# Loads moved twelve slots ahead, residual sums moved to VectorE, whole columns moved to ScalarE at the seams of a two-block transformer kernel

## The reference

```python
for i in range(DEPTH):                                  # DEPTH = 2
    need_ctx = i < DEPTH - 1
    xl = _rmsnorm(hl, norm1_g[i]) * (1.0 + ml[:, :, 1]) + ml[:, :, 0]
    xc = _rmsnorm(hc, norm1_g[i]) * (1.0 + mc[1]) + mc[0]
    yl, yc = mixer(xl, xc)                              # even: mLSTM + attention, odd: window attention
    hl = hl + ml[:, :, 2] * yl
    xl = _rmsnorm(hl, norm2_g[i]) * (1.0 + ml[:, :, 4]) + ml[:, :, 3]
    hl = hl + ml[:, :, 5] * _peer_ffn(xl, ...)          # routing, then 128 x 128 experts, all computed
    if need_ctx:
        hc = hc + mc[2] * yc
        xc = _rmsnorm(hc, norm2_g[i]) * (1.0 + mc[4]) + mc[3]
        hc = hc + mc[5] * _peer_ffn(xc, ...)
return _rmsnorm(hl, final_g)
```

## Time and profile before

| what | value |
|---|---|
| median of 3 runs | 4660.26 us (4651.77 to 4663.33) |
| the profiled execution: its time, its span | 4653.44 us, 4651.6 us |
| mean granted TensorE clock | 0.934 |
| busy: TensorE, VectorE, ScalarE, GpSimd | 4128.3, 3019.9, 2105.6, 375.1 us |
| TensorE's idle time before seams 2 and 3 | 14.5 us, 14.4 us |

### The profile page before, as it was taken

One profiled execution on the slowest core, in us unless ns is written; L12 is line 12 of the kernel. 1 busy time (PEld: TensorE's weight loads), 2 busy tenths in 40 slices (PEclk: granted clock), 3 DMA queues, 4 the chain that ended last, 5 costly groups with the idle time before them and its releaser, 6 DMA issues. The chain is left out here.

```text
span 4651.6 us, 71198 instructions
## 1 busy us (share of the span) xinstructions
PE 4128.3 (89%) x25056; PEld 3615.7 (78%) x25056; DVE 3019.9 (65%) x5902; ACT 2105.6 (45%) x3230; POOL 375.1 (8%) x462
## 2 busy tenths in 40 slices
PE   6987999869886766999999879999997769999998
PEld 5985889758774656888888668888886568888887
DVE  4555555455527448877777697777775578777776
ACT  4433444344423224555555445555554445555554
POOL 0000000000000004400000053000001035000000
PEclk9997999889975887999999889999998989999999
DMA  5555555545410112255555423555554031555554
GB/s 193 185 194 197 204 206 188 202 179 182 149 57 30 47 68 98 73 189 189 189 189 190 175 73 111 191 191 192 190 189 155 32 118 37 190 190 190 190 191 168
DMA packets 105283, 718.10 MB, mean 154 GB/s; under 512 B 13856, under 2 KB 14464, under 8 KB 21280
## 3 DMA queue, kind: packets, MB, share of 16 engines
q1 hardware_dynamic: 94544, 659.35, 39.8%
q0 software_dynamic: 8880, 52.12, 2.9%
q10 hardware_dynamic: 1696, 4.46, 0.3%
HBM read 709.48 MB, written 6.39 MB: 154 GB/s over the span
## 5 line engine op out<-in xcount | busy, mean ns | idle before, releaser
L228 DVE TENSOR_TENSOR units<-ring,units 128x1024 fp32r<-128x1024 f32 x1158 | 1408.6, 1225 | 598.8 <-ACT units L221 598.5
L221 ACT ACTIVATE units<-ring 128x1024 fp32r<-128x1024 f32 x1206 | 1273.0, 1056 | 1043.4 <-PE ps L251 998.3
L2868 PE MATMUL ps<-wide,units 128*128 128x512 f32 x3072 | 759.0, 389 | 3.0 <-PEq L2766 3.0
L2868 PEld LDWEIGHTS ps<-wide,units 128*128 128x128 f32 x3072 | 576.2, 188 | 122.8 <-issue 3.5
L249 PE MATMUL ps<-units,weighted 128*128 128x512 f32 x1536 | 603.8, 393 | 8.7 <-DVE units L228 8.7
L250 PE MATMUL ps<-units,weighted 128*128 128x512 f32 x1536 | 602.8, 392 | 0.0
L251 PE MATMUL ps<-units,weighted 128*128 128x512 f32 x1536 | 598.3, 389 | 0.0
L2919 ACT ACTIVATE low_halves<-ps 128x256 f32<-128x256 f32 x384 | 147.8, 385 | 685.7 <-PE ps L2870 685.7
L2870 PEld LDWEIGHTS ps<-wide,units 128*128 128x128 f32 x3072 | 419.1, 190 | 29.9
L2870 PE MATMUL ps<-wide,units 128*128 128x256 f32 x3072 | 428.3, 282 | 0.0
L2937 DVE TENSOR_TENSOR gelued<-low_halves,ps 128x256 f32<-128x256 f32 x384 | 161.9, 422 | 376.3 <-ACT low_halves L2919 376.3
(11 more groups left out here) (495 smaller groups left out, 6531.3 us busy)
## 6 DMA issues: line engine op xcount, KB each, us to landing
ring<-in_stream SPq DMA_DIRECT2D x603, 1024.0 KB, 4.8
quad_ring<-in_mod_w POOLq DMA_DIRECT2D x12, 4096.0 KB, 13.8
front<-residuals_dram SPq DMA_DIRECT2D x5, 1024.0 KB, 7.2
gain_rows<-in_norm_gains SPq DMA_DIRECT2D x6, 512.0 KB, 4.6
peer_keys<-in_keys SPq DMA_DIRECT2D x3, 1024.0 KB, 5.3
ml_mask<-in_ml_mask ACTq DMA_DIRECT2D x1, 2048.0 KB, 7.8
residuals_dram<-residual SPq DMA_DIRECT2D x2, 1024.0 KB, 6.6
front<-mod_rows_dram SPq DMA_DIRECT2D x4, 512.0 KB, 7.9
```

Source lines behind the costliest of these rows:

```text
L221: act.activation(K.parts(n)[0], K.raw(n), ACT.Copy).then_inc(K.sig("hi_made").sem, 1)
L228: dve.tensor_tensor(lo, K.raw(n), hi.bitcast(FP32), ALU.subtract).then_inc(K.sig("unit_split").sem, 1)
L2868: pe.matmul(both, hi[:, k, :], pair[:, :, k, :], start=(k == 0), stop=False)
```

## The change

1. In `experts` SP issues the stage's loads when the slots up to twelve before the end have been issued, and the last slots after them.
2. In `RouteHead` ScalarE makes the whole column from PSUM (`whole_scalar`), which frees the bank; VectorE makes high and low parts from it in SBUF (`parts_vector`), for columns 0 to 3, then 4 to 7.
3. VectorE adds the residual that GpSimd added, behind the columns; of that residual's two gate products one stands before the columns and one between columns 3 and 4. TensorE waits for each of them only before the chunk that writes its banks (`wait_banks`).
4. In `OddHead` the context rows' sum and norm stand between the two unit splits for chunk 1. Their columns 0 to 3 are made after chunk 1, 4 to 7 after chunk 2.

```diff
-        return (self.whole_made if self.pooled else self.low_made).at(n)
+        return self.whole_made.at(n)
...
+def whole_scalar(K, act, E):
+    for k in range(KD):
+        act.wait_ge(*E.turned.at(k + 1))
+        if k >= E.whole.shape[1]:
+            act.wait_ge(*E.low_made.at(k - E.whole.shape[1] + 1))
+        act.activation(E.whole[:, k % E.whole.shape[1], :], E.bank(K, k), ACT.Identity, bias=E.shift[:, k:k + 1],
+                       scale=E.gain[:, k:k + 1]).then_inc(E.whole_made.sem, 1)
+
+
+def parts_vector(K, dve, E, columns):
+
+    n = E.whole.shape[1]
+    for k in columns:
+        dve.wait_ge(*E.whole_made.at(k + 1))
+        dve.tensor_copy(E.pair[:, 0, k, :], E.whole[:, k % n, :]).then_inc(E.high_made.sem, 1)
+        dve.wait_ge(*E.high_made.at(k + 1))
+        dve.tensor_tensor(E.pair[:, 1, k, :], E.whole[:, k % n, :], E.pair[:, 0, k, :].bitcast(FP32), ALU.subtract)\
+           .then_inc(E.low_made.sem, 1)
...
-        high_parts(self.K, act, self.E, range(KD))
+        whole_scalar(self.K, act, self.E)
...
-        low_parts_vector(K, dve, self.E)
+        parts_vector(K, dve, self.E, range(4))
+        if other is not None:
+            gate_products(K, dve, other, range(1, MT))
+        parts_vector(K, dve, self.E, range(4, KD))
+        if other is not None:
+            add_products(K, dve, other)
...
-        for S in self.sums:
-            pe.wait_ge(*S.made.at(MT))
...
+        pe.wait_ge(*self.below.made.at(t + 1))
...
+    def between_vector(self, dve, c):
+        if c == 0:
+            add_products(self.K, dve, self.total)
+            prepare_vector(self.K, dve, self.ctx)
+
+    def late_vector(self, dve, c):
+        if c in (1, 2):
+            whole_columns(self.K, dve, self.ctx, range(4 * c - 4, 4 * c))
...
-    def late_tensor(self, pe):
-        turn_tensor(self.K, pe, self.ctx)
+    def late_tensor(self, pe, c):
+        if c in (1, 2):
+            turn_tensor(self.K, pe, self.ctx, range(4 * c - 4, 4 * c))
...
-                split_ahead(K, eng, split, K.taken + c + 1)
-            if c == 0 and late is not None:
-                late(eng)
+                split(K, eng, 2 * (K.taken + c + 1))
+                if head is not None:
+                    between(eng, c)
+                split(K, eng, 2 * (K.taken + c + 1) + 1)
+            if head is not None:
+                late(eng, c)
...
-                head.gpsimd(pool)
...
-                stream_weights(K, sp, KEYS)
+                stream_weights(K, sp, KEYS - 12)
                 sp.wait_ge(weights_made.sem, weights_made.base + STEPS * 4 * FRONT)
                 for dst, src, signal in loads:
                     sp.dma_start(dst, src).then_inc(signal.sem, 16)
+                stream_weights(K, sp, KEYS)
```

More of the change, by code:

```diff
@@ L679, with __init__ @@
 class RouteHead:
[L683 to L685 removed]
+    def __init__(self, K, E, ahead, mine, other=None):
+        self.K, self.E, self.ahead, self.mine, self.other = K, E, ahead, mine, other
+        self.sums = [S for S in (mine, other) if S is not None]
+        self.below = self.sums[-1]
     def scalar(self, act):
@@ L717, in sync_end @@
         K = self.K
[L718 to L719 removed]
+        if self.other is not None:
+            store_sum(K, sp, self.other)
         for S in self.sums:
```

86 lines of the change are left out of this document (34 added, 52 removed).

## The result

The changed kernel takes 4603.2 us (median of 4 executions, 4602.6 to 4605.4), the kernel before 4660.6 us (4 executions, 4651.8 to 4663.3). The ratio is 0.988, with a 95% interval of 0.986 to 0.990.

What follows compares the result with a forecast made beforehand. A pass was taken as bound by TensorE, the seams by the residual's transfer, the routing by VectorE. Terms 22.6 + 4.0 + 4.8 + 6.7 + 1.8 = 39.9 us off the 4660.3 median gave 4620 us, range 4606 to 4636.

Steps and rivals of the forecast that it cites:

- The loads (22.6): After the first and second passes, early loads end the squares' wait for the residual: 11.3 us each, 22.6 in all.
- the disturbance: Mid-pass loads delaying the slot stream: taken as 0, at the bad end 7 us in each of three passes.
- a collision: Rival: mid-pass loads delay slots beyond their spare time, taking 21 us away, 4641 us; chance 0.08.
- a ring that falls behind: Rival: each pass's last nine slots land late one after another, 130 us less 40, 4750 us; chance 0.02.
- the loads are not what holds the seam: Rival: squares wait for something behind the load, early loads give nothing, 17.3 us left, 4643 us; chance 0.03.
- Seam 2 (4.0): Between first and second pass: quicker columns bring first scores 5.8 us earlier, less charges 4.0 us, bounds 2 and 6.
- 1.3 for the taking of turns: Between first and second pass: charge of 1.3 us for VectorE's sums and GpSimd's next unit excluding each other.
- 0.5 for the clock: Between first and second pass: charge of 0.5 us for the routing's first matmuls running at half clock.
- the first rival: VectorE and GpSimd take turns fully, costing 2.4, 1.1 and 1.2 us in seams 1, 2, 3: 4625 us; chance 0.15.
- Seam 1 (4.8): Ahead of the first pass: VectorE's norm gains 2.8 and 1.0 us, the columns 1.0; together 4.8, bounds 3 and 7.
- Seam 3 (6.7): After the second pass: chunk 1 no longer waits for the context rows' norm and turns, 6.7 us, bounds 4 and 8.
- Seam 4 (1.8, bounds 0 and 3.4): Ahead of the third pass: first matmul 2 us earlier, but more of the first chunk at half clock, 1.8 us.

Runs made afterwards that it cites:

- loads_only: Kernel before, only with the next stage's loads issued twelve slots ahead of the pass's end: 4633.5 us against 4655.1 for before.
- warm_short: Changed kernel plus 22 idle transposes on TensorE behind the last product of a pass: 4609.1 us.
- vector_units: Changed kernel with the low halves of the routing's first two units made by VectorE instead of GpSimd: 4606.9 us.
- late_norm: Changed kernel with the context rows' norm, turns and columns back in one piece behind chunk 0 in seam 3: 4612.9 us.
- before_dense: Kernel before plus idle transposes filling in part TensorE's waits between the turns of seam 4: 4656.9 us.
- pool_sums: Changed kernel with the second residual's sums in seams 1 and 2 handed back from VectorE to GpSimd: 4614.8 us.
- norm_and_units: Changed kernel with the next rows' norm in the pass's last four steps and the routing's first two low halves on VectorE: 4604.0 us.
- after_again: Changed kernel word for word, run in more executions: 4606.7 us against 4656.3 for before, ratio 0.989.
- loads_late: Changed kernel with the loads put back behind the whole slot stream: 4635.7 us.
- norm_in_pass: Changed kernel with the next rows' norm moved from behind the pass's last splits into its last four steps: 4607.4 us.

## Why the prediction was right and wrong

**The loads (22.6).** Right: 22.9 in the changed kernel and 23.0 with the loads alone. The first two passes did not lose anything (709.04 and 709.09 us, 709.06 and 709.07), so taking 0 for the disturbance was right, and the rivals of a collision and of a ring that falls behind are out. So is the one in which the loads are not what holds the seam (loads_only gives 22.8 us in the two gaps).

**Seam 2 (4.0).** Measured 5.5. The order of events was as worked out: first matmul at 3.6 us behind the turn (I had 4.3), GpSimd's unit ready at 11.3 (11.5), first scores at 17.8 (17.4 without charges). What failed is the charges: 1.3 for the taking of turns and 0.5 for the clock. The turns were taken in full, as the first rival says, and the sums took 4.60 us together instead of 2.4. The page "SBUF — State Buffer" of the Trainium skill has it so (section "Who interferes with whom"): a VectorE instruction with two SBUF inputs and a GpSimd instruction that reads SBUF contend for a shared pair of ports, which is an exclusive lock. The trace agrees with that rule: each waited for the other's instruction to end (3.47 us for a sum of 1.2, 3.19 for a unit of 2.4). Its price is not in the time of this seam, for two reasons: behind the sums VectorE waits anyway, and TensorE, at half clock for 21 matmuls of the first chunk (7.84 us for its 48, as before the change), comes to GpSimd's unit only when it is ready. At full clock, in warm_short, it waits 1.4 us for it. The clock charge was nothing because the chunk ran as long at half clock before.

**Seam 1 (4.8).** Measured 7.0, at its bound. 3.8 us of it come ahead of the first turn, as many as the 2.8 and 1.0 that I had for the norm (mean 0.17 and scaling 1.42 us, as forecast). Behind the turn I took 1.0; it is 3.2. 1.8 of them come up to the first score matmul: the first product matmul is 2.2 us earlier (4.25 us behind the turn instead of 6.46) and the first chunk's 48 take 6.27 us instead of 6.87, but then TensorE waits for GpSimd's unit, for which it did not wait before:

```profile
PE ps L249 <- POOL units L228: 1.3, 1, 1.3
```

Here the taking of turns has a price: that unit takes 3.17 us instead of 2.43, and vector_units, without the wait, has the first score matmul 1.0 us earlier. So the first rival was right in kind for seam 1, at 0.7 to 1.0 us instead of its 2.4. The other 1.4 us come at the routing's end, where the 64 small matmuls that turn the gates ran at half clock before and mostly at full clock now (seam 4 has the same):

```profile
1842.90:1850.70 7.80, 6.85 (x64) 6.59 (x64) 5.60 (x5) 0.49 (x1) 0.00 (x0) 0.50 0.01 2
```

```profile
1834.50:1840.80 6.30, 5.11 (x59) 4.77 (x60) 5.65 (x5) 0.49 (x1) 0.00 (x0) 0.75 0.01 3
```

**Seam 3 (6.7).** Measured 5.3, and 4.7 by late_norm. Chunk 1 has no wait longer than 1 us (0.5 for a unit) and a group of turns takes about 1.0 us, as forecast, and chunk 0 ends 1.0 us later, where I charged up to 1.2. 7.2 us are won by the end of the four chunks (7.7 by late_norm), so the term was right and a little small. 1.9 are given back in the window attention behind them, which no edit touches: its first 17 us ran at a clock of 0.97 before and run at 0.73 now.

```profile
3645.00:3662.00 17.00, 11.77 (x78) 7.39 (x77) 11.77 (x38) 11.30 (x24) 0.00 (x0) 0.97 0.00 1
```

```profile
3600.00:3617.00 17.00, 13.79 (x70) 9.16 (x70) 10.97 (x34) 10.10 (x23) 0.00 (x0) 0.73 0.00 1
```

**Seam 4 (1.8, bounds 0 and 3.4): the step that failed.** Measured 6.0. I had written "First matmul 2 us earlier, but more of the first chunk at half clock". The first half is right, 2.4 us. The second has the wrong sign. I let the full clock come back at the same time behind the wait as before, so that work moved forward would fall into the half clock. The trace shows that the half clock ends sooner when the gaps between the turns are smaller: 3.2 us behind the first turn instead of 10.4, and before_dense moves it to 3.6 with nothing but filler. It is worth 1.7 us in the first chunk, so that 4.1 us are won up to the first scores where I had 1.8. The end is not fixed by the turns alone: of the ten traces with the new columns in seam 4, six have it at 3.2 us and four at 5.0 to 5.7, with first scores 0.5 to 0.7 us later (late_norm, pool_sums, warm_short, norm_and_units). Another 1.9 us come at the end of the routing, most of it where the gates are turned, and 1.5 in the third pass, whose first 10 us ran at 0.83 before and at full clock now:

```profile
3936.00:3946.00 10.00, 10.00 (x42) 8.25 (x41) 6.32 (x12) 4.39 (x7) 0.00 (x0) 0.83 0.52 179
```

```profile
3888.90:3898.90 10.00, 10.00 (x53) 8.56 (x52) 7.16 (x11) 4.76 (x8) 0.00 (x0) 1.00 0.64 215
```

These two pieces are no merit of one edit: other runs (late_norm, pool_sums, warm_short) have the 1.6 us in the third pass again, and before_dense, with the third pass of before, does not have them, though nothing there differs in the code. I can name what they are, stretches of half clock that begin or end at another place, but what decides each of them stays open.

**The sum (39.9, bounds 31.6 and 47).** Measured 48.1 in the part that the edits can reach, above the bound. Seam 4 makes 4.2 of the difference of 8.2, seam 1 2.2, the third pass 1.5, seam 2 1.5 and the loads 0.3; seam 3 takes 1.4 back. The sharing of VectorE and GpSimd, which I gave 0.15 as a rival and a charge in the forecast, was real, free in seam 2 and cost 0.7 to 1.0 us in seam 1. The clock, which I charged half a microsecond, was the largest of what I missed: it gave 0.6 and 1.4 us in seam 1, 1.7 and 1.9 in seam 4 and 1.5 in the third pass, and took 1.9 in seam 3, some 5 us in all, worked out from the matmuls' distances and the stretches above.

**The base.** I set the sum against the median of three executions of before, 4660.3, and allowed some 4 us for their scatter. 15 executions have their median at 4656.3. The other 9 of the 57 us are scatter between executions. 2.6 of them can be seen in the first 1740 us of the two profiled executions, which the change doesn't touch, and 7 lie between the profiled execution of before and its median; that these, too, come from this part is likely, since the rest repeats within 0.1 us where it was traced twice, but only one execution of each run is profiled. With 4656.3 and 39.9 the forecast would have been 4616, and 4608 with the 48.1 measured, where after_again has 4606.7.

**Small slips in the working.** 48 matmuls take 5.7 us at full clock because they start 0.12 us apart; the 19 that stand in the row of 2 us would give 5.1, since matmuls overlap the ends of a stretch. TensorE's gap in front of chunk 1 was 10.0 us (3573.55 to the first product at 3583.55), not 10.3. 4608 to 4634 follows with half of the 11.6 us added at each end; with 4 us it is 4609 to 4633. None of these moves the forecast by more than 0.3 us or the range by more than 1.4.

## What to carry to other kernels

When the profile names a transfer as the releaser of a wait, and the queue was free long before, issue it where the queue has room: the gain is the wait, and it could be read off beforehand to 0.2 us for each of the two (11.3 for 11.5 and 11.4). Where an edit closes gaps in TensorE's work behind a wait, count the clock as part of the gain, read from the granted clock of short stretches on both sides, and look at which GpSimd operation the earlier work will now meet, since a step that comes 0.3 us sooner can land in front of a longer one, as in before_dense. Before a sum of small terms is set against a median, look at how far an untouched part of the program scatters: here by 14 us, more than any single term but one.

## What the runs showed of the hardware

- Filling gaps of 0.3 to 0.7 us between turns in part with idle transposes (1.6 us of waiting became 1.1) brought TensorE's full clock back 3.6 us behind the first turn instead of 10.4. A gap of 3 us at full clock was followed by a stretch at half clock, which began only 1.6 us behind the turn that ended the gap and lasted until 8.4; with 0.6 us instead of 3 there was none. Behind a gap of 14.5 us (loads_late) the same turns began at half clock, but the full clock was back after 3.9 us.
- At the end of a pass a wait of 1.09 us for a unit left the clock at 1.00, and one of 1.84 us (norm_in_pass) was followed at once by eight matmuls at half clock.
- Outside the places of an edit, passes of 709 us agree within 0.1 us between traces (709.01 to 709.09), or take 1.6 us more (710.62 to 710.69), and nothing between. An edit that gains 1 us somewhere can therefore cost or give 1.6 us elsewhere, as vector_units and warm_short did.
- A GpSimd subtraction of 128x1024 that starts just before a VectorE subtraction of 128x256 makes it last 2.3 to 2.6 us instead of 0.41, for each of two in a row where GpSimd has two units to do (before_dense).
